# Inverting the chunks of a gated delta rule: 64 columns a level in place of 128

## The chip, the cores and the metric

The kernel runs on one core of a Trainium2 chip. Its time is the device time of one execution in microseconds (us); the median of three runs of the kernel before is 3099.11 us (3098.83 to 3103.76). A core has TensorE (PE: matrix products into the PSUM banks; its weight loads are listed apart as PEld), VectorE (DVE), ScalarE (ACT), GpSimd (POOL), SyncE (SP) and DMA queues. Engines run on their own and wait for each other on semaphores.

## The reference, cut to what matters

One inference step of a two-layer decoder. The first layer is a gated DeltaNet layer of 8 heads on 1024 prompt tokens (and 8 sample tokens), the second a dilated window attention; each is followed by an MLP. In the delta rule the tokens are cut into chunks, and in each chunk a unit lower triangular matrix is inverted:

```python
lower = jnp.where(strict, jnp.einsum('...ik,...jk->...ij', kb, kc) * decay, 0.0)
eye = jnp.broadcast_to(jnp.eye(C, dtype=jnp.float32), lower.shape)
T = lax.linalg.triangular_solve(eye + lower, eye, left_side=True, lower=True, unit_diagonal=True)
u = jnp.einsum('...ij,...jv->...iv', T, vc * bc[..., None])
```

Then a recurrence runs over the chunks with a 128x128 state. All arithmetic is float32.

## The kernel before, in words

The kernel uses chunks of 128 tokens (8 per head, `CH`), which gives the same result as the reference's chunks of 64. For each of the 8 heads each engine runs three functions one after the other: `front` (norms, key products, transposes), `levels` (the inversion) and `recurrence`. TensorE's own order is written out by hand in the program; between the small products of all three functions it runs pieces of the large projection for the next head (`dense`, lines 1854 to 1856: three products of 352 or 328 columns per step), so that it has something to do while the others work. The last head has no such pieces, and has the work for the sample tokens instead (`samples_update`, L1895 on TensorE, L1206 on VectorE).

`levels` inverts by doubling: the inverse of blocks of size b = 2, 4, ..., 64 is known, and a level joins two neighbours of size b into one of 2b (`LEVELS` = 6). `inv` holds the inverse of the 8 chunks, `inv_t` its transpose, `low` the triangular matrices, `blk` what `low` has between the two neighbours of the level (masked by `lvl`), `prod` the first product. The chunks go in two halves h of four chunks, with a PSUM bank for each half. In one level:

- TensorE, L1972 by way of `four` (L1961): for each chunk `blk`^T times `inv`, a float32 product of 128x128 with 128 columns, into bank 3 + h. From level 2 on it also transposes `inv` (L1974, recorded at L1779). Then one step of `dense`.
- ScalarE, L678: copies the bank to `prod`; L683: copies the transpose to `inv_t`.
- TensorE, L1982: `inv_t`^T times `prod` into bank 6 - h (at the last level L1984: `prod`^T times `inv_t` into banks 7 and 3). Then one step of `dense`.
- VectorE, L1317: the next level's `blk`; L1323: subtracts the second product from `inv` (at the last level from `inv_t`). At levels 1 to 4 it also makes the low part of a weight tile (L930), after ScalarE made the high part (L500).

A float32 product appears in the trace as two weight loads and two matmul records; a product of the projection (fp32r) or a transpose as one of each. The first product of level 1 waits for `blk` of L1300, the last step of VectorE's `front`. After level 6 the recurrence waits for the zeroed `state` (L1379), which VectorE writes after its last L1323.

Of the kernel before, what the change touches and what calls it, by code (L numbers as in the profile page):

```python
# [19 lines left out]
ALU = mybir.AluOpType  # L20
# [3 lines left out]
P = 128  # L24
# [150 lines left out]
def build(nc, t):  # L175
# [4 lines left out]
    def sem(name):  # L180
        if name not in made:
            made[name] = ctx.enter_context(nc.semaphore(name))
        return made[name]
# [172 lines left out]
    def hc(h):  # L356
        return slice(4 * h, 4 * h + 4)
# [11 lines left out]
    def conv_out(head, n):  # L369
        return qk(head, n) if n < 2 else v_conv[:]  # L370

    def slots_of(head):
        return ((0, 1), (2, 3))[head % 2]

# [117 lines left out]
    def _(act):  # L492
# [180 lines left out]
        def levels(head):  # L673
            last = head == HEADS - 1
            for level in range(1, LEVELS + 1):
                for h in range(2):
                    act.wait_ge(sem(f"bank{3 + h}_full"), L.next(f"bank{3 + h}_full"))
                    act.activation(prod[:, hc(h)], psum[:, 3 + h].rearrange(four, n=P), ACT.Copy  # L678
                    ).then_inc(sem(f"bank{3 + h}_free"), L.add(f"bank{3 + h}_free"))
                    if level > 1:  # L680
                        b = (7, 5)[h]
                        act.wait_ge(sem(f"bank{b}_full"), L.next(f"bank{b}_full"))
                        act.activation(inv_t[:, hc(h)], psum[:, b].rearrange(four, n=P), ACT.Copy  # L683
                        ).then_inc(sem(f"bank{b}_free"), L.add(f"bank{b}_free"))
                skip(*((6, 5) if level < LEVELS else (7, 3)))
                if not last and level <= 4:
                    which, part = divmod(level - 1, 2)
                    split_hi(2 * head + 4 + which, slots_of(head)[which], (part,))
                if level == 5:
                    act.activation(s_z[:, head], z_g[:, SEQ:NT], ACT.Copy).then_inc(sem("act_order"), L.add("act_order"))  # L690
                    act.activation(z_g[:, 0:SEQ], z_g[:, 0:SEQ], ACT.Silu).then_inc(sem("z_ready"), L.add("z_ready"))
                if last and level == 2:
                    act.wait_ge(sem("s_rows_full"), L.next("s_rows_full"))
                    act.activation(s_rows[:], psum[0:HEADS * NS, 1, 0:2 * P].rearrange("p (k n) -> p k n", n=P), ACT.Copy
                    ).then_inc(sem("s_rows_ready"), L.add("s_rows_ready"))
                    act.wait_ge(sem("s_out_sums_full"), L.next("s_out_sums_full"))
                    act.activation(s_u[:, 6], psum[:, 0, 320:384], ACT.Sqrt, scale=1.0 / P / P, bias=eps[:, 0:1]
                    ).then_inc(sem("s_rms_ready"), L.add("s_rms_ready"))
            if last:
                act.wait_ge(sem("act_order"), L.value("act_order"))  # L700
                act.activation(s_z[:], s_z[:], ACT.Silu).then_inc(sem("s_z_ready"), L.add("s_z_ready"))
# [217 lines left out]
    def _(dve):  # L919
# [387 lines left out]
        def levels(head):  # L1307
            last = head == HEADS - 1
            blk, inv = blk_of(head), inv_of(head)
            for level in range(1, LEVELS + 1):  # L1310
                for h in range(2):
                    v.wait_ge(sem(f"bank{3 + h}_full"), L.next(f"bank{3 + h}_full"))
                    L.skip(f"bank{3 + h}_free")
                if level > 1:
                    skip(7, 5)
                if level < LEVELS:
                    v.tensor_tensor(blk, low[:], o3(lvl[:, level + 1], CH), ALU.mult  # L1317
                    ).then_inc(sem("blocks_ready"), L.add("blocks_ready"))
                v.wait_ge(sem(L.last), L.value(L.last))
                for h in range(2):  # L1320
                    b, to = ((7, 3)[h], inv_t) if level == LEVELS else (6 - h, inv)
                    v.wait_ge(sem(f"bank{b}_full"), L.next(f"bank{b}_full"))
                    v.tensor_tensor(to[:, hc(h)], to[:, hc(h)], psum[:, b].rearrange(four, n=P),  # L1323
                                    ALU.subtract).then_inc(sem(f"bank{b}_free"), L.add(f"bank{b}_free"))
                if not last and level <= 4:
                    which, part = divmod(level - 1, 2)
                    split_lo(2 * head + 4 + which, slots_of(head)[which], (part,))
                if level == 5:
                    v.wait_ge(sem("q_squares_ready"), L.next("q_squares_ready"))
                    for h in range(2):  # L1330
                        v.tensor_reduce(col[:, 1, hc(h)], v_conv[:, halves[h]].rearrange(four, n=P), AXX, ALU.add
                        ).then_inc(sem("dve_order"), L.add("dve_order"))
                    v.wait_ge(sem(L.last), L.value(L.last))
                    v.tensor_scalar(col[:, 4], col[:, 1], EPS, None, ALU.add).then_inc(sem("dve_order"), L.add("dve_order"))
                    v.wait_ge(sem(L.last), L.value(L.last))
                    v.reciprocal(col[:, 11], col[:, 4]).then_inc(sem("dve_order"), L.add("dve_order"))
                if not last and level == 5:
                    take_product(0, head + 1)
                if last and level == 2:
                    samples_values()  # L1340
                if last and level > 2:
                    samples_update(level - 3)
            v.wait_ge(sem(L.last), L.value(L.last))
# [396 lines left out]
    def _(pe):  # L1740
# [217 lines left out]
        def four(bank, h, lhs, rhs):  # L1958
# [2 lines left out]
                done = mm(psum[:, bank, c * P:(c + 1) * P], lhs[:, 4 * h + c], rhs[:, 4 * h + c], start=True, stop=True)  # L1961
            done.then_inc(sem(f"bank{bank}_full"), L.add(f"bank{bank}_full"))

        def levels(head):
            last = head == HEADS - 1
            blk, inv = blk_of(head), inv_of(head)
            at_step = 24
            for level in range(1, LEVELS + 1):
                pe.wait_ge(sem("blocks_ready"), L.next("blocks_ready"))
                for h in range(2):  # L1970
                    peek((5, 7)[h] if level == 1 else 6 - h)
                    four(3 + h, h, blk, inv)  # L1972
                    if level > 1:
                        transposes((7, 5)[h], [inv[:, 4 * h + c] for c in range(4)])  # L1974
                dense(head, at_step, at_step + 1)
                if level == 1:
                    pe.wait_ge(sem("inverse_t_ready"), L.next("inverse_t_ready"))
                for h in range(2):
                    peek(3 + h)
                    peek((7, 5)[h])  # L1980
                    if level < LEVELS:
                        four(6 - h, h, inv_t, prod)  # L1982
                    else:
                        four((7, 3)[h], h, prod, inv_t)  # L1984
                dense(head, at_step + 1, at_step + 2)
                at_step += 2
                if last and level == 1:
                    pe.wait_ge(sem("s_qk_ready"), L.next("s_qk_ready"))
                    pe.wait_ge(sem("s_state_landed"), L.next("s_state_landed", 32))
                    for n in range(HEADS * NS):  # L1990
                        mm(psum[:, 0, 128 + 2 * n:130 + 2 * n], s_state[n // 32][:, n // NS % 4, n % NS], s_u[:, 0:2, n],
                           start=True, stop=True)
                    mm(psum[:, 0, 256:320], ones[:], s_u[:, 2], start=True, stop=True
                    ).then_inc(sem("s_reads_full"), L.add("s_reads_full"))
                if last and level == 2:
                    pe.wait_ge(sem("s_v_ready"), L.next("s_v_ready"))
                    mm(psum[0:HEADS * NS, 1, 0:P], s_u[:, 1], ident[:], start=True, stop=True)
                    mm(psum[0:HEADS * NS, 1, P:2 * P], s_u[:, 5], ident[:], start=True, stop=True
                    ).then_inc(sem("s_rows_full"), L.add("s_rows_full"))
                    pe.wait_ge(sem("s_out_squares_ready"), L.next("s_out_squares_ready"))  # L2000
                    mm(psum[:, 0, 320:384], ones[:], s_u[:, 7], start=True, stop=True
                    ).then_inc(sem("s_out_sums_full"), L.add("s_out_sums_full"))
                if last and level > 2:
                    samples_update(level - 3)
# [333 lines left out]
```

## Time and profile before

| | before |
|---|---|
| median of 3 runs | 3099.11 us |
| the profiled execution | 3105.82 us, its span 3104.0 us |
| mean granted TensorE clock | 0.951 of full speed |
| TensorE busy | 2853.4 us (92%) |
| TensorE weight loads busy | 2779.5 us (90%) |
| VectorE busy | 1664.5 us (54%) |
| ScalarE busy | 858.4 us (28%) |
| DMA | 165.99 MB, mean 53 GB/s |

The span runs from the first to the last instruction. Busy time counts a stretch once however many instructions overlap in it. Matmul records overlap, so what one costs in a stream is the distance between starts, not its own duration. The granted clock (PEclk) is 1.00 at 2.4 GHz and 0.50 at 1.2 GHz. The eight heads (counted from 0) take the stretch from about 84 to about 930 us.

### The profile page before, as it was taken

To read this page: it belongs to the slowest core of one execution; us is meant where nothing else is said; L and a number is where in the kernel's file an instruction comes from. 1 tells how busy PE (TensorE), PEld (TensorE's weight loads), DVE (VectorE), ACT (ScalarE), POOL (GpSimd) and SP (SyncE) were. 2 spreads that over 40 slices of the span, in tenths; PEclk is the share of its full clock that TensorE was granted. 3 is DMA by queue.
4 is the path that set the end of the run, shared out by engine and by line. 5 is a ranking of instruction groups with operands and counts; after the bars stand their busy time and mean duration, and the time that the engine had idled before them with its cause. 6 is when DMAs were issued, how large, how long until landed. Compare 5 with 4: busy or idle time off the path is not lost. (4 is left out here: it accounts for less than half of the span.)

```text
span 3104.0 us, 47551 instructions
## 1 busy us (share of the span) xinstructions
PE 2853.4 (92%) x18652; PEld 2779.5 (90%) x18652; DVE 1664.5 (54%) x3124; ACT 858.4 (28%) x1907; POOL 30.2 (1%) x20
## 2 busy tenths in 40 slices
PE   5999999999777999999999999668849999999998
PEld 2999999999747999999999999658739999999997
DVE  4766677766334644444444653257857444444445
ACT  3544344434112311122111320125514111122111
POOL 0000000000020000000000000000000000000000
PEclk8999999999768999999999999879969999999999
DMA  3100011002113111111111113721231111111111
GB/s 113 55 16 29 29 35 36 29 15 83 62 55 106 55 41 41 54 41 54 41 46 49 41 65 95 68 76 56 76 115 41 55 41 41 54 41 54 41 41 55
DMA packets 102203, 165.99 MB, mean 53 GB/s; under 512 B 47081, under 2 KB 65809, under 8 KB 101604
## 3 DMA queue, kind: packets, MB, share of 16 engines
q1 hardware_dynamic: 59604, 142.35, 14.2%
q10 hardware_dynamic: 42464, 21.74, 3.3%
q8 instruction: 98, 1.61, 0.2%
q14 instruction: 37, 0.30, 0.0%
HBM read 134.63 MB, written 34.67 MB: 55 GB/s over the span
## 5 line engine op out<-in xcount | busy, mean ns | idle before, releaser
L1752 PE MATMUL psum<-x_hi,w_hi 128*128 128x352 f32 (+1 forms) x2128 | 685.8, 322 | 13.4 <-DVE w_lo L930 6.5
L1753 PE MATMUL psum<-x_lo,w_hi 128*128 128x352 f32 (+1 forms) x2128 | 681.2, 320 | 0.0
L1754 PE MATMUL psum<-x_hi,w_lo 128*128 128x352 f32 (+1 forms) x2128 | 677.9, 319 | 0.0
L1752 PE MATMUL psum<-u_hi,w_hi 128*128 128x352 f32 (+1 forms) x1632 | 525.4, 322 | 2.4 <-DVE u_lo L1726 2.4
L1753 PE MATMUL psum<-u_lo,w_hi 128*128 128x352 f32 (+1 forms) x1632 | 522.8, 320 | 0.0
L1754 PE MATMUL psum<-u_hi,w_lo 128*128 128x352 f32 (+1 forms) x1632 | 521.2, 319 | 0.0
L1752 PEld LDWEIGHTS psum<-x_hi,w_hi 128*128 128x128 f32 x2128 | 400.5, 188 | 17.4 <-DVE x L1441 8.7
L1753 PEld LDWEIGHTS psum<-x_lo,w_hi 128*128 128x128 f32 x2128 | 401.0, 188 | 0.7
L1754 PEld LDWEIGHTS psum<-x_hi,w_lo 128*128 128x128 f32 x2128 | 400.7, 188 | 0.0
L776 ACT ACTIVATE u_hi<-relu 128x352 fp32r<-128x352 f32 (+1 forms) x192 | 94.4, 492 | 1047.0 <-DVE relu L1472 1047.0
L1441 DVE TENSOR_TENSOR x<-x,psum 128x352 f32<-128x352 f32 x336 | 170.8, 512 | 363.5 <-PE psum L1754 363.5
L500 ACT ACTIVATE w_hi<-w_raw,gains 128x512 fp32r<-128x512 f32 x384 | 249.2, 712 | 238.6 <-DMA w_raw<-in_w 128.9
L1752 PEld LDWEIGHTS psum<-u_hi,w_hi 128*128 128x128 f32 x1632 | 307.7, 189 | 3.2 <-issue 2.8
L1753 PEld LDWEIGHTS psum<-u_lo,w_hi 128*128 128x128 f32 x1632 | 308.3, 189 | 0.4
L1754 PEld LDWEIGHTS psum<-u_hi,w_lo 128*128 128x128 f32 x1632 | 307.6, 188 | 0.0
L930 DVE SCALAR_TENSOR_TENSOR w_lo<-w_raw,gains,w_hi 128x512 fp32r<-128x512 f32 x384 | 264.0, 746 | 39.3 <-ACT w_hi L500 39.0
L1854 PE MATMUL psum<-x_hi,w_hi 128*128 128x352 f32 (+1 forms) x768 | 273.0, 355 | 12.7 <-issue 10.1
L1855 PE MATMUL psum<-x_lo,w_hi 128*128 128x352 f32 (+1 forms) x768 | 247.5, 322 | 0.0
L1856 PE MATMUL psum<-x_hi,w_lo 128*128 128x352 f32 (+1 forms) x768 | 247.0, 322 | 0.0
L1469 DVE SCALAR_TENSOR_TENSOR relu<-psum,rs 128x352 f32<-128x352 f32 (+1 forms) x192 | 99.1, 516 | 221.5 <-PE psum L1754 216.7
L1854 PEld LDWEIGHTS psum<-x_hi,w_hi 128*128 128x128 f32 x768 | 147.3, 192 | 13.0 <-issue 10.2
L1475 DVE TENSOR_TENSOR u_lo<-relu,u_hi 128x352 fp32r<-128x352 f32 (+1 forms) x192 | 99.3, 517 | 107.1 <-ACT u_hi L776 107.1
(296 smaller groups left out, 3549.7 us busy)
## 6 DMA issues: line engine op xcount, KB each, us to landing
w_raw<-in_w SPq DMA_DIRECT2D x192, 512.0 KB, 3.7
scratch_att<-o_out ACTq DMA_DIRECT2D x48, 132.0 KB, 2.6
q_tile<-scratch_q SPq DMA_DIRECT2D x24, 256.0 KB, 2.9
merge<-scratch_att SPq DMA_DIRECT2D x8, 768.0 KB, 4.7
scratch_q<-q_stage ACTq DMA_DIRECT2D x24, 176.0 KB, 2.3
x<-in_x SPq DMA_DIRECT2D x8, 516.0 KB, 8.1
scratch_o_heads<-head_out ACTq DMA_DIRECT2D x8, 512.0 KB, 2.7
s_state<-in_s_rec_in ACTq DMA_DIRECT2D x2, 2048.0 KB, 10.3
```

Source lines behind the costliest of these rows:

```text
L500: done = act.activation(w_hi[:, slot, 2 * part + k], w_raw[:, part, k], ACT.Copy, scale=gains[:, bass.ds(unit * UW + 2 * part + k, 1)])
L776: act.activation(u_hi[:, tile, THIRDS[third]], relu[:, 0:width(third)], ACT.Copy).then_inc(sem("u_hi_ready"), L.add("u_hi_ready"))
L930: done = v.scalar_tensor_tensor(w_lo[:, slot, 2 * part + k], w_raw[:, part, k], gains[:, bass.ds(unit * UW + 2 * part + k, 1)], f(w_hi[:, ...
L1441: v.tensor_tensor(out, out, psum[:, TAKES[n % 6], 0:width(third)], ALU.add).then_inc(sem("product_free"), L.add("product_free"))
L1469: v.scalar_tensor_tensor(r, psum[:, TAKES[n % 6], 0:width(third)], 0.0, rs[:, cols], ALU.max, ALU.mult).then_inc(sem("product_free"), L.ad ...
L1475: v.tensor_tensor(u_lo[:, tile, cols], r, f(u_hi[:, tile, cols]), ALU.subtract).then_inc(sem("u_ready"), L.add("u_ready"))
L1752: mm(out, whi, xh[:, k, cols], start=k == 0, stop=False)
L1753: mm(out, whi, xl[:, k, cols], start=False, stop=False)
L1754: done = mm(out, wlo, xh[:, k, cols], start=False, stop=k == kts - 1)
L1854: mm(out, whi, x_hi[:, k, cols], start=k == 0, stop=False)
L1855: mm(out, whi, x_lo[:, k, cols], start=False, stop=False)
L1856: done = mm(out, wlo, x_hi[:, k, cols], start=False, stop=k == KT - 1)
```

## The change

The inverse is block triangular. At a level with block size b only the columns of the even blocks (64 of 128) of each chunk's `inv` change. The new kernel computes only these. `upper` picks them: runs of b columns, with b columns left out between them. The first product takes them as moving operand and puts them side by side in the bank; ScalarE copies 64 columns per chunk in place of 128; the second product takes 64 columns; VectorE subtracts 64 columns into the same runs of `inv`. At the last level the roles are swapped: the stationary operand is the 64 columns of `prod`, the moving operand the right half of `inv_t`, and the output 64 partitions with 64 columns. The stationary operand of all other products (`blk`, `inv_t`) stays 128x128. The transposes of `inv`, the copy to `inv_t`, the masks and the order of all instructions stay as they are, and no wait is added or removed.

```diff
+    def upper(ap, level):
+
+        b = 2 ** level
+        return ap.rearrange("p c (n m) -> p c n m", m=2 * b)[:, :, :, 0:b]
...
-                    act.activation(prod[:, hc(h)], psum[:, 3 + h].rearrange(four, n=P), ACT.Copy
+                    act.activation(prod[:, hc(h), 0:P // 2], psum[:, 3 + h, 0:HALF // 2].rearrange(four, n=P // 2), ACT.Copy
                     ).then_inc(sem(f"bank{3 + h}_free"), L.add(f"bank{3 + h}_free"))
...
-                    b, to = ((7, 3)[h], inv_t) if level == LEVELS else (6 - h, inv)
+                    b = (7, 3)[h] if level == LEVELS else 6 - h
                     v.wait_ge(sem(f"bank{b}_full"), L.next(f"bank{b}_full"))
-                    v.tensor_tensor(to[:, hc(h)], to[:, hc(h)], psum[:, b].rearrange(four, n=P),
-                                    ALU.subtract).then_inc(sem(f"bank{b}_free"), L.add(f"bank{b}_free"))
+                    if level < LEVELS:
+                        to = upper(inv[:, hc(h)], level)
+                        new = psum[:, b, 0:HALF // 2].rearrange("p (c n m) -> p c n m", c=4, m=2 ** level)
+                    else:
+                        to = inv_t[0:P // 2, hc(h), P // 2:P]
+                        new = psum[0:P // 2, b, 0:HALF // 2].rearrange(four, n=P // 2)
+                    v.tensor_tensor(to, to, new, ALU.subtract).then_inc(sem(f"bank{b}_free"), L.add(f"bank{b}_free"))
...
+        def halves_of(bank, h, level, lhs, rhs):
+
+            pe.wait_ge(sem(f"bank{bank}_free"), L.next(f"bank{bank}_free"))
+            for c in range(4):
+                cols = slice(c * P // 2, (c + 1) * P // 2)
+                if rhs is not prod and lhs is not prod:
+                    moving = upper(rhs[:, 4 * h + c:4 * h + c + 1], level).rearrange("p c n m -> p (c n) m")
+                    out = psum[:, bank, cols].rearrange("p (n m) -> p n m", m=2 ** level)
+                    done = mm(out, lhs[:, 4 * h + c], moving, start=True, stop=True)
+                elif rhs is prod:
+                    done = mm(psum[:, bank, cols], lhs[:, 4 * h + c], rhs[:, 4 * h + c, 0:P // 2], start=True, stop=True)
+                else:
+                    done = mm(psum[0:P // 2, bank, cols], lhs[:, 4 * h + c, 0:P // 2], rhs[:, 4 * h + c, P // 2:P],
+                              start=True, stop=True)
+            done.then_inc(sem(f"bank{bank}_full"), L.add(f"bank{bank}_full"))
...
-                    four(3 + h, h, blk, inv)
+                    halves_of(3 + h, h, level, blk, inv)
...
-                        four(6 - h, h, inv_t, prod)
+                        halves_of(6 - h, h, level, inv_t, prod)
                     else:
-                        four((7, 3)[h], h, prod, inv_t)
+                        halves_of((7, 3)[h], h, level, prod, inv_t)
```

## Rows read from the trace of the kernel before

**Rows 1.** Waits of TensorE, 84 to 785 us: engine, line, releaser: us, times, longest.
```profile
PE psum L1961 <- DVE pair L1300: 15.4, 7, 2.2
PE psum L2021 <- DVE state L1379: 3.9, 7, 0.6
```
**Rows 2.** Windows, head 1: levels, then the rest: PE, PEld, DVE, ACT, POOL, PEclk, DMA.
```profile
222.56:255.00 32.44, 31.88 (x269) 31.60 (x269) 22.59 (x33) 17.96 (x32) 0.00 (x0) 1.00 0.22 66
255.00:317.00 62.00, 59.80 (x430) 59.51 (x431) 43.30 (x88) 24.04 (x62) 0.00 (x0) 1.00 0.03 10
```
**Rows 3.** Timeline of TensorE, one level of head 2: start, us, engine, line, count.
```profile
321.85 1.05 PE L1961 MATMUL psum<-pair 128*128 128x128 f32 x8
322.74 0.60 PE L1779 MATMUL psum<-ident,pair 128*128 128x128 f32 x4
323.18 1.06 PE L1961 MATMUL psum<-pair 128*128 128x128 f32 x8
...
325.00 1.95 PE L1961 MATMUL psum<-dec,inv_t 128*128 128x128 f32 x16
326.70 0.41 PE L1854 MATMUL psum<-x_hi,w_hi 128*128 128x352 f32 x1
```
**Rows 4.** Timeline of TensorE, four short streams with other operand sizes.
```profile
42.87 3.57 PE L1793 MATMUL psum<-ones,sq_sum 128*128 128x1 f32 x16 [4.93 <-DVE sq_sum L952]
52.01 0.60 PE L1871 MATMUL psum<-x,w_ab 128*16 128x8 f32 x16
802.67 27.44 PE L1991 MATMUL psum<-s_u,s_state 128*128 128x2 f32 x128 [6.86 <-DMA s_state<-in_s_rec_in]
1026.18 0.71 PE L1806 MATMUL psum<-ones,sq_sums 128*88 128x1 f32 x8
1026.75 0.39 PE L1752 MATMUL psum<-x_hi,w_hi 128*128 128x328 f32 x1
```
**Rows 5.** Timeline of TensorE, the last head's level 1.
```profile
789.91 3.62 PE L1961 MATMUL psum<-pair 128*128 128x128 f32 x16
793.32 2.49 PE L1961 MATMUL psum<-dec,inv_t 128*128 128x128 f32 x16
```
**Rows 6.** Groups of VectorE and ScalarE in the heads: count, busy us, mean ns, idle before.
```profile
L1323 DVE TENSOR_TENSOR pair<-pair,psum 128x512 f32<-128x512 f32 x70 | 48.1, 688 | 25.3 <-PE psum L1961 20.1
L1277 DVE TENSOR_TENSOR low<-psum,pair 128x256 f32<-128x256 f32 x32 | 13.3, 414 | 0.3 <-PE psum L1921 0.2
L678 ACT ACTIVATE dec<-psum 128x512 f32<-128x512 f32 x96 | 57.3, 597 | 182.0 <-PE psum L1961 182.0
L694 ACT ACTIVATE s_rows<-psum 64x256 f32<-64x256 f32 x1 | 0.4, 377 | 3.5 <-PE psum L1998 3.5
```
**Rows 7.** Timeline of TensorE, from level 6 to the recurrence, head 2.
```profile
346.65 1.95 PE L1961 MATMUL psum<-inv_t,dec 128*128 128x128 f32 x16
348.36 0.41 PE L1854 MATMUL psum<-x_hi,w_hi 128*128 128x352 f32 x1
```
**Rows 8.** Timeline of TensorE, first product of four heads' levels.
```profile
127.91 2.95 PE L1961 MATMUL psum<-pair 128*128 128x128 f32 x16 [2.20 <-DVE pair L1300]
222.56 2.05 PE L1961 MATMUL psum<-pair 128*128 128x128 f32 x16 [2.20 <-DVE pair L1300]
315.60 2.91 PE L1961 MATMUL psum<-pair 128*128 128x128 f32 x16 [2.20 <-DVE pair L1300]
410.26 2.05 PE L1961 MATMUL psum<-pair 128*128 128x128 f32 x16 [2.20 <-DVE pair L1300]
```
**Rows 9.** Windows: after the gap of head 2, twice; then the sample products; the last recurrence.
```profile
316.60:320.00 3.40, 3.40 (x17) 3.40 (x16) 1.23 (x1) 2.05 (x4) 0.00 (x0) 0.50 0.02 7
320.00:349.60 29.60, 29.08 (x247) 28.79 (x245) 20.57 (x30) 15.91 (x29) 0.00 (x0) 1.00 0.24 72
802.70:830.10 27.40, 27.40 (x129) 27.40 (x129) 0.00 (x0) 0.00 (x0) 0.00 (x0) 0.50 0.00 1
880.00:925.00 45.00, 40.18 (x95) 22.68 (x93) 16.69 (x43) 4.96 (x22) 14.97 (x8) 0.50 0.16 63
```
**Rows 10.** Windows: the last head's levels 2 to 6.
```profile
835.50:876.40 40.90, 32.77 (x196) 25.80 (x194) 18.24 (x28) 12.91 (x24) 14.98 (x8) 0.87 0.07 26
```

## The prediction

> **What bounds the kernel now.** I read the waits of TensorE first, since it is busy 92% of the span. Between 84 and 785 us, seven heads long, it waits for VectorE twice per head and for next to nothing else: 2.20 us at the door of the levels and about 0.56 us at the door of the recurrence, 19.3 us in 700 [rows 1]. The windows say the same: in a head's levels TensorE is busy 31.88 of 32.44 us, while VectorE has 22.59 and ScalarE 17.96 [rows 2]. So in seven heads the time is the length of TensorE's own stream. What an operation costs there is the distance from its first start to the next group's start: in a level, 8 records of the first product take 0.89 us, 4 transposes 0.44, 16 records of the second product 1.70 [rows 3]: 107 to 111 ns a record. The last head has no projection to fill in, and there TensorE also waits for VectorE [rows 10].
>
> **The change part by part.** *The products.* Per head 6 levels x 2 halves x 4 chunks x 2 products x 2 records = 192 records get 64 moving columns in place of 128. Does a record get shorter? The trace has streams with nearly no moving columns. With a 128-column stationary operand, 128 records of 2 moving columns take 27.3 us (802.67 to 829.97), 213 ns each, at a granted clock of 0.50 [rows 4, 9]. At the same clock 16 records of 128 moving columns take 3.41 us, 213 ns each [rows 5]. Sixteen records of 1 column with 128 stationary columns: the last ends 3.57 us after the first began [rows 4], the same pace. At full clock 8 records with 88 stationary columns and 1 moving take 0.57 us, 71 ns each, which is 88/128 of 107 less 2 ns; and with 16 stationary columns and 8 moving a record costs under 38 ns (0.60 us for 16) [rows 4]. So the pace of these records goes by the stationary columns: the weight load takes the whole slot, and the moving columns run inside it. 176 of the 192 records keep 128 stationary columns, and I forecast 107 to 111 ns for them, as before. The bounds for one record: 107 (all load) and 53 (half). I take the upper end, because two streams of 1 and 2 columns lie on it and 64 is between them and 128. What is unseen is a moving operand in runs of 2 or 4 elements with gaps: it has half the slot as slack, so even at twice the time per column it costs nothing; at four times, levels 1 and 2 would cost 64 records x 0.1 us x 8 heads = 26 us at most.
>
> The 16 records of the second product at level 6 have 64 stationary and 64 moving columns: 107 ns becomes 53, 0.86 us per head at full clock.
>
> The Trainium skill (TensorE: Matmul & The Clock Gate, "Back-to-back issue gap") has the gap between matmuls shrink with the moving columns, down to about 60 cycles at 64. By that alone all 192 records would halve; it is the third rival below. The trace's streams of 1 and 2 columns disagree with it for float32 operands with 128 stationary columns [rows 4].
>
> *The copies and subtractions.* L1323 goes from 688 ns to that of L1277, which also takes 256 elements from a bank: 414. 12 of them per head: 3.3 us less of VectorE. L678 goes from 597 towards 377 (L694, 256 elements): 2.6 us less of ScalarE per head [rows 6]. Both lie beside TensorE's stream, which doesn't wait for them [rows 1], so they are worth nothing in seven heads but for one place: after level 6 TensorE waits for L1379, which stands behind the last two L1323. There the second product ends 0.86 us sooner, the step of the projection behind it still takes its time [rows 7], and VectorE is 0.27 us faster per subtraction: I take 0.27 us per head (0 to 0.55). If the runs of 2 elements double the price of a subtraction, it is 0.83 us, near the 0.69 of before, and stays hidden. Nothing is added, moved or made to wait.
>
> So a head gains 0.86 + 0.27 = 1.13 us so long as the clock stays. The 2.20 us at the door of the levels stay too: their releaser is in `front`.
>
> *The clock.* This is the term that decides. At the door of the levels TensorE stands 2.20 us, in all seven heads alike. In four of them (the first, third, fifth and seventh) the granted clock then falls to 0.50: the first product is 2.9 us long in place of 2.05 [rows 8]. About 1 us after that product's start the clock is down, and after 3.4 us of back-to-back work it is up again and stays for the level [rows 9]. A fall costs 1.61 us (the heads' first products lie 94.65, 93.04, 94.66 us apart) [rows 8]. What brought it back was a stream of full 128-column and 352-column records. Other streams don't bring it back, though TensorE is busy: 27.40 us busy out of 27.40 at 0.50 with 2 moving columns, and the last recurrence, 40.18 busy out of 45.00 at 0.50, with gaps and half-filled products [rows 9]. After the change the levels are such a stream: of the 10 us that a level takes at half clock, 6.8 are records whose moving columns fill half their slot. I forecast that a fall at the door now lasts through all levels, until the recurrence with its many 352-column records raises the clock. Also, a fall becomes likelier, since what follows the gap is thin too.
>
> The Trainium skill (same page, "Part 1: The HAM clock gate") says that matmul activity releases the throttle and asks to keep TensorE busy. If busy time as the profile shows it were that activity, the clock would come back within the levels as before; this is the second rival. The rows of 27.40 and 40.18 busy us at 0.50 speak against it.
>
> Price of one fall: the levels hold 31.88 us of TensorE's work [rows 2]. At half clock all of it doubles except the 16 records that halved: (31.9 - 1.7) x 2 + 1.7 = 62.1, so +30.2. Less 1.0 before the clock is down; plus some 5 us (3 to 7) of recurrence still at half clock, +2.5; less 0.3 at the recurrence's door: +31.4 us.
>
> How many falls? Before, four of seven, in strict alternation, because the heads are of nearly equal length. A head that is 31 us longer and others 1.1 us shorter break that pattern. The same 2.20 us made the clock fall at one door and not at the next, so something that the rows don't show decides. I take three of seven, next to the four of the rows, and one to five as bounds.
>
> *The last head.* Its level 1 ends long before the sample state lands (6.86 us of waiting) [rows 4] and can get slower for nothing. From there it starts at half clock; now the first full records raise the clock, 0.87 on average over levels 2 to 6, which means 30 of 40.9 us at full clock, some 24 of them busy [rows 10]. With thin records it stays down: at most +24. VectorE's shorter subtractions on the chain to L1895 give back 2. I take +17 (10 to 24).
>
> Sum: 3 x 31.4 = +94.3; the four falls of before gone, -6.4; four heads at full clock, 4 x 1.13 = -4.5; last head +17: **+100 us**. The profiled execution, 3105.8 us, would be 3206; it is 6.7 above the median of the runs, against which the forecast is 3099.1 + 100 = 3199 us.
>
> **The rivals.**
> - *The clock falls, but comes back within the levels*, helped by the transposes and the projection's steps: a third of a level's time at half clock is filled with full records. Then a fall costs perhaps 10 us: 3 x 10 + 10 for the last head - 14 = +26, 3125 us.
> - *The clock behaves as before* (busy time is what counts). Then only the gains are left: 8 x 0.86 + 8 x 0.27 = 9, and 2 of VectorE's chain in the last head: -11, 3088 us, faster. For it: the levels' stream has no gap. Against: rows 9. It decides from the point where no door's fall outlasts the few us of now.
> - *Records halve with their columns*: 1408 more records save 50 ns each, -70, together 3018 us. Against: rows 4.
> - *Runs with gaps are slow to read or write*: +26 at most, inside the forecast's range.
>
> **How the numbers follow.** Forecast 0.74; clock comes back within the levels 0.08; clock as before 0.12; records halve 0.06. A measurement of this kernel tells 0.2%, 6 us. Faster: the last two, less a little, 0.17. Same, 0.06: no fall at any door and the last head's +17 against -11 of gains. Slower 0.77. With one to five falls the forecast itself reaches from 3130 to 3260, and single executions should differ by tens of us, since the door's gap decides anew in each. The range is 3088 to 3250: it takes in the clock as before, and leaves out halved records and more than four or five falls.
>
> **What would show it.** Right: starts of the 64-column records 107 to 111 ns apart at full clock and 213 at half, level 6's second product 53 and 107; long stretches of PEclk 0.50 over whole `levels`, about 64 us long in place of 32.4, and a lower mean clock (0.951 now, near 0.92); L1323 near 414 ns; executions of one kernel that differ by more than the 5 us of now. Wrong: a level of under 5 us at full clock (records did halve), or PEclk 0.50 for only some 3 us behind each door.

## The result and the profile after

The changed kernel takes 3131.41 us (median of four runs, 3126.46 to 3142.18), the kernel before 3101.44 (3098.83 to 3105.89): ratio 1.010, 95% interval 1.0067 to 1.0133. It is slower by 30 us. The forecast was slower by 100. Its four runs lie 15.7 us apart, those of before 7.1. The profiled executions below (3105.82 and 3142.18 us) are at the long end of both kernels.

| | before | after |
|---|---|---|
| the profiled execution | 3105.82 us | 3142.18 us |
| its span | 3104.0 us | 3140.4 us |
| mean granted TensorE clock | 0.951 | 0.933 |
| TensorE busy | 2853.4 us | 2895.9 us |
| VectorE busy | 1664.5 us | 1635.6 us |
| ScalarE busy | 858.4 us | 845.9 us |

TensorE has less to stream and is busy for longer. Where, the windows of the changed kernel say, from the first product of the levels to the first product of the recurrence, one line for each head (stretch, its length, PE, PEld, DVE, ACT and POOL busy with counts, PEclk, DMA share, GB/s):

```profile
127.84:173.33 45.49, 45.24 (x268) 44.83 (x268) 19.39 (x33) 16.48 (x32) 0.00 (x0) 0.66 0.16 47
233.95:271.36 37.41, 37.16 (x268) 36.75 (x268) 19.40 (x33) 16.49 (x32) 0.00 (x0) 0.82 0.20 57
331.99:367.79 35.80, 35.56 (x268) 35.14 (x268) 19.40 (x33) 16.49 (x32) 0.00 (x0) 0.86 0.19 60
428.41:465.82 37.41, 37.16 (x268) 36.75 (x268) 19.39 (x33) 16.49 (x32) 0.00 (x0) 0.82 0.19 57
526.44:560.63 34.19, 33.94 (x268) 33.53 (x268) 19.39 (x33) 16.48 (x32) 0.00 (x0) 0.90 0.20 62
621.25:652.22 30.97, 30.72 (x268) 30.30 (x268) 19.40 (x33) 16.49 (x32) 0.00 (x0) 1.00 0.23 69
712.83:750.26 37.43, 37.18 (x268) 36.76 (x268) 19.39 (x33) 16.49 (x32) 0.00 (x0) 0.82 0.49 169
814.84:919.10 104.26, 90.19 (x386) 78.62 (x386) 19.27 (x39) 15.38 (x30) 14.97 (x8) 0.52 0.14 56
```

The same windows of the kernel before, for a head without a fall of the clock, one with (there are three and four of them), and the last head:

```profile
222.31:254.74 32.43, 31.87 (x268) 31.58 (x268) 22.67 (x33) 17.96 (x32) 0.00 (x0) 1.00 0.22 66
315.35:349.39 34.04, 33.48 (x268) 33.19 (x268) 22.67 (x33) 17.96 (x32) 0.00 (x0) 0.95 0.21 64
...
789.66:880.58 90.92, 73.88 (x386) 65.29 (x385) 24.77 (x39) 17.29 (x30) 14.98 (x8) 0.71 0.16 64
```

The head with PEclk 1.00 is 1.46 us shorter than before (30.97 against 32.43). In the six others the clock falls. A length times (1 - PEclk) times 2 gives the time at half clock: 31, 13, 10, 13, 7, 0 and 13 us, 88 in all, against 14 before. What it costs is what a window has above 30.97: 14.5, 6.4, 4.8, 6.4, 3.2, 0 and 6.5 us, 41.9 in all, a little under half of the 88 us. The four falls of before cost 4 x 1.61 = 6.4, and the shorter stream gives back 7 x 1.46 = 10.2, so the seven windows are 41.9 - 6.4 - 10.2 = 25.3 us longer (258.7 us in all). The last head's levels are 13.3 us longer, and the stretch behind them 2.1 us shorter. Together that is the 36.4 us by which the span grew.

The three other executions of the changed kernel have mean clocks of 0.936 to 0.939 against 0.933 in the profiled one. By their spans this is 20 to 40 us less at half clock (an estimate; where in the kernel, no run shows). So what is read from this profile is the upper end of what the change costs: 36 us, where the medians say 30.

The timeline of TensorE in the changed kernel shows parts of two levels at half clock (first five lines, head 0), then a whole level at full clock, then level 6's second product (start, us, engine, line, count):

```profile
135.38 1.80 PE L1982 MATMUL psum<-pair 128*128 128x64 f32 x8
136.97 1.06 PE L1789 MATMUL psum<-ident,pair 128*128 128x128 f32 x4
137.82 1.81 PE L1982 MATMUL psum<-pair 128*128 128x64 f32 x8
...
151.24 3.51 PE L1984 MATMUL psum<-dec,inv_t 128*128 128x64 f32 x16
154.51 0.64 PE L1864 MATMUL psum<-x_hi,w_hi 128*128 128x352 f32 x1
...
163.20 1.00 PE L1982 MATMUL psum<-pair 128*128 128x64 f32 x8
164.04 0.61 PE L1789 MATMUL psum<-ident,pair 128*128 128x128 f32 x4
...
166.26 1.89 PE L1984 MATMUL psum<-dec,inv_t 128*128 128x64 f32 x16
167.96 0.41 PE L1864 MATMUL psum<-x_hi,w_hi 128*128 128x352 f32 x1
168.52 1.00 PE L1982 MATMUL psum<-pair 128*128 128x64 f32 x8
...
171.67 1.15 PE L1986 MATMUL psum<-inv_t,dec 128*64 128x64 f32 x16
172.74 0.43 PE L1864 MATMUL psum<-x_hi,w_hi 128*128 128x352 f32 x1
```

At full clock 8 records with 64 moving columns take 0.84 us (163.20 to 164.04) where 8 with 128 took 0.89 [rows 3]; 16 of the second product take 1.70 us, as before. A whole level takes 5.32 us (163.20 to 168.52) against 5.41. Half the columns are gone, and 0.09 us of 5.41 with them. At half clock 8 records take 1.59 us (135.38 to 136.97), 199 ns each, and 16 of the second product 3.27 (151.24 to 154.51), 204 ns each.

### The profile page after: what moved, and what is told of

Read it like the earlier page. It is cut to its first block and busy times, and to the rows that moved or that the text cites. A ratio compares the mean times of both kernels' runs of the same rounds, so it can differ in the third digit from the quotient of the medians.

```text
span 3140.4 us, 47551 instructions
## 1 busy us (share of the span) xinstructions
PE 2895.9 (92%) x18652; PEld 2818.3 (90%) x18652; DVE 1635.6 (52%) x3124; ACT 845.9 (27%) x1907; POOL 30.1 (1%) x20
## 3 DMA queue, kind: packets, MB, share of 16 engines
q8 instruction: 98, 1.61, 0.2%
```

## The experiments

Each was timed beside the kernel before on the same chip; ratios are to that.

**1. The gap at the door filled, changed kernel.** Four steps of the projection, which the recurrence had, are issued where TensorE stands idle.

```diff
+DOOR = 4
...
-            at_step = 24
+            at_step = 24 + DOOR
+            dense(head, 24, at_step)
...
-            start = 24 + 2 * LEVELS
+            start = 24 + DOOR + 2 * LEVELS
```

> The changed kernel, with four of the projection's steps moved from the recurrence to the door of the levels, where TensorE stands 2.20 us idle in each of seven heads. Theory (the slowdown is the clock, which falls at that idle stretch and which the thin records then hold down): four steps are 1.9 us, so 0.3 us of idling is left, the clock doesn't fall in heads 0 to 6, their levels run at full clock, 1.5 us shorter than before, and the idle time filled gives 1.9 us more per head: 7 x -3.4 = -24 us against the kernel before, +13 for the last head, which has no projection to fill in: about 3090 us. Rival (records with gaps in their moving operand, or the small copies, cost the time): the clock may rise, but the time stays at 3131 less 13, near 3118.

Measured: 3093.09 us (3085.05 to 3094.71) beside 3107.85 before, ratio 0.9943 (0.9929 to 0.9956). The windows of the levels, first of seven like ones and the last head:

```profile
129.19:160.15 30.96, 30.71 (x268) 30.29 (x268) 19.40 (x33) 16.51 (x32) 0.00 (x0) 1.00 0.24 69
...
761.02:865.55 104.53, 90.59 (x386) 79.11 (x385) 19.29 (x39) 15.40 (x30) 14.97 (x8) 0.52 0.14 56
```

PEclk is 1.00 in all seven heads, and the same thin stream (one whose records have few moving columns for the slot of 128) takes 30.96 us there. So 64-column records alone didn't make the clock fall in these heads; the idle stretch was needed for it, though it was not enough by itself: in the changed kernel one of seven doors kept the clock, before the change three. The last head, with no step to fill in, is as long as in the changed kernel. The slowdown of the seven heads is the clock's, and not that of the operands with gaps. Beside their own times before, the changed kernel is 30 us slower with the gap and 15 us faster without it: 45 us, some 6 per door.

**2. The same move in the kernel before.**

> The kernel before with the same move of four steps, the control for the first run. Theory: the idle time filled gives 7 x 1.9 = 13 us, and the four falls of the clock (1.6 us each) go: -20, about 3081 us, so the first run is then some 10 us above this one, all of it from the last head. Rival (the recurrence lacks the four steps and waits there): 3095 to 3101 us, with new waits of TensorE in the recurrence.

Measured: 3088.73 us (3087.27 to 3091.03), ratio 0.9940 (0.9926 to 0.9953): 19 us faster than before. Its seven windows are 32.42 or 32.43 us long at PEclk 1.00, so the four falls are gone. In its waits of TensorE the door is down to 1.9 us in total for seven heads, and the recurrence shows no new wait:

```profile
PE psum L2023 <- DVE state L1380: 3.9, 7, 0.6
PE psum L1962 <- DVE pair L1301: 1.9, 7, 0.3
```

The move is worth 19 us alone, as expected (20; the absolute 3081 was missed because the kernel before ran 6 us longer beside these runs). The change adds nothing to it: the seven heads gain 10 us by the change and the last head loses 13.8 (104.53 against 90.73). The first run is 4.4 us above this one by medians. I had expected some 10, because my expectation for the first run left out the four falls that go.

**3. Level 1 at 128 columns, the rest of the change kept.** In all three engines `level == 1` takes the old form.

```diff
-                    halves_of(3 + h, h, level, blk, inv)
+                    if level == 1:
+                        four(3 + h, h, blk, inv)
+                    else:
+                        halves_of(3 + h, h, level, blk, inv)
```

> The changed kernel, but level 1, which lies right behind the idle stretch, keeps its 128 columns in both products, the copy and the subtraction. Theory: the full records of level 1 bring the clock back as they did before (3.4 us at half clock per fall), and levels 2 to 6 are thin at full clock: falls in about four of seven heads, at 1.6 us each; seven heads 9 us shorter than before, the last head 13 longer: about 3105 us. Rival (the clock comes back only in the projection's and the transposes' records, whatever level 1 does): 3125 to 3131 us and 10 us at half clock per head.

Measured: 3109.26 us (3102.36 to 3112.93, 11 runs), ratio 1.0003 (0.9994 to 1.0012). The windows: five heads like the first line, two like the second, then the last head:

```profile
129.13:160.09 30.96, 30.71 (x268) 30.30 (x268) 19.93 (x33) 16.93 (x32) 0.00 (x0) 1.00 0.21 69
...
403.89:436.44 32.55, 32.30 (x268) 31.88 (x268) 19.93 (x33) 16.93 (x32) 0.00 (x0) 0.95 0.23 65
...
777.68:875.22 97.54, 82.63 (x386) 73.54 (x385) 21.02 (x39) 15.82 (x30) 14.97 (x8) 0.59 0.15 59
```

A fall costs 1.6 us again, as before the change. In this execution one full level behind the gap was enough to bring the clock back, and five thin levels after it then ran at full clock. The last head is 6.6 us longer than before, not the 13 expected. This profile is of the shortest of the eleven executions; most of the others have lower mean clocks (down to 0.944 against 0.948), so they had more or longer stretches at half clock, and the median is 7 us above it. Even so, the median of all eleven is 1 us above the kernel before, where the changed kernel's is 30.

**4. VectorE's part alone.** All products and copies at 128 columns, the subtraction on 64.

```diff
+                    bank = psum[:, b].rearrange(four, n=P)
+                    if level < LEVELS:
+                        to, new = upper(to[:, hc(h)], level), upper(bank, level)
+                    else:
+                        to, new = to[0:P // 2, hc(h), P // 2:P], bank[0:P // 2, :, P // 2:P]
```

> The kernel before with VectorE's part alone: all products and the copies at 128 columns, the subtraction L1323 on the 64 columns that change. Theory: a subtraction takes about 414 ns in place of 688; worth 0.5 us per head at the recurrence's door and 2 us on the chain of the last head: 3096 us, mean clock 0.95 as before. Rival (subtractions in runs of 2 elements are slow): L1323 over 688 ns at levels 1 and 2, and no gain.

Measured: 3100.93 us (3096.36 to 3106.00) beside 3107.85, ratio 0.9974 (0.9964 to 0.9985), clock 0.953. The levels are 32.15 us long against 32.43, the last head's 89.18 against 90.92. That is 2.0 and 1.7 us of the 6.9; and in its profile two doors fell, not four, which is 3.2 us more by way of the clock. So the expected 0.5 us per head at the recurrence's door was 0.28. The subtraction takes 421 ns here (413 at level 6) in place of 688. The shortest and the longest of the 80 at levels 1 to 5 are 414 and 432 ns, so runs of 2 elements cost no more than runs of 32. The changed kernel's groups of VectorE show the same times:

```profile
L1334 DVE TENSOR_TENSOR pair<-pair,psum 128x256 f32<-128x256 f32 x70 | 29.5, 421 | 51.4 <-PE psum L1984 51.3
L1334 DVE TENSOR_TENSOR inv_t<-inv_t,psum 64x256 f32<-64x256 f32 x14 | 5.5, 413 | 13.0 <-PE psum L1986 13.0
```

**5. The parts that pay, together.** The kernel before with the door filled, VectorE's part, and of the products only level 6's second:

```diff
+        def corner(bank, h):
...
+                done = mm(psum[0:P // 2, bank, c * P // 2:(c + 1) * P // 2], prod[:, 4 * h + c, 0:P // 2],
+                          inv_t[:, 4 * h + c, P // 2:P], start=True, stop=True)
```

> The kernel before with the parts that the first runs showed to be worth something: four projection steps at the door, VectorE's subtraction on 64 columns, and level 6's second product as 64 stationary and 64 moving columns; all other products and the copies stay at 128 columns, so that no record is thin for its slot. Theory: the door-filled kernel before (3088.7) less 7 for VectorE's part and 8 x 0.86 for level 6: 3075 us, levels of heads 0 to 6 33.6 us long, no fall of the clock there, the last head's levels no longer than before (94 us). Rival (thin records save something themselves, so that leaving 11 of 12 products full loses it): no better than the door-filled changed kernel, 3090.

Measured: 3073.23 us (3072.53 to 3075.30) beside 3103.68, ratio 0.9905 (0.9889 to 0.9920). It is 30 us faster than before. The changed kernel with its door filled was 15 us faster than its own before, so this one is 12 (by the ratios) to 16 us (by the medians) better; the two ran on different chips, and their times can't be subtracted directly. Levels, first of seven like ones, and the last head:

```profile
127.27:158.71 31.44, 31.20 (x268) 30.78 (x268) 19.39 (x33) 17.97 (x32) 0.00 (x0) 1.00 0.24 68
...
762.50:851.15 88.65, 72.43 (x386) 64.60 (x385) 21.51 (x39) 17.20 (x30) 14.97 (x8) 0.73 0.16 64
```

A level stretch is 0.48 us longer than the all-thin one (30.96), and the last head 15.9 us shorter. The time came out as expected (3075), the parts less so: level 6's second product gives 0.63 us and not 0.86, and the last head's levels are 2.3 us shorter than before. The 33.6 us expected for a level stretch compare with 31.44 plus the 1.9 of the four steps, which stand ahead of this window.

**6. 32 moving columns.** The changed kernel with both products of levels 1 to 5 and the first of level 6 at 32 columns; half of what a level changes is left out.

```diff
...
-                    done = mm(psum[:, bank, cols], lhs[:, 4 * h + c], rhs[:, 4 * h + c, 0:P // 2], start=True, stop=True)
+                    done = mm(psum[:, bank, c * P // 2:c * P // 2 + P // 4], lhs[:, 4 * h + c], rhs[:, 4 * h + c, 0:P // 4],
+                              start=True, stop=True)
```

> The changed kernel with 32 moving columns in place of 64 in both products of levels 1 to 5 and in the first of level 6 (it leaves out half of what each level changes). Theory (the pace goes by the stationary columns, and how thin the records are decides how long the clock stays down): records at full clock still 107 to 111 ns apart; falls at about as many doors, but each now lasts to the end of the levels, some 30 us lost per fall: 3150 to 3250 us, and runs far apart. Rival 1 (the pace goes by the moving columns after all, with a floor): records under 90 ns apart and a shorter level. Rival 2 (the clock comes back by time or by busy share alone): falls as long as in the changed kernel, about 14 us at half clock, 3131 us.

Measured: 3283.07 us (3279.24 to 3289.52), ratio 1.0574 (1.0558 to 1.0591). The two kinds of head alternate, and none keeps the clock; then TensorE's timeline inside one:

```profile
128.71:185.09 56.38, 56.14 (x267) 55.64 (x268) 19.44 (x33) 16.51 (x32) 0.00 (x0) 0.52 0.13 38
245.71:303.18 57.47, 57.22 (x268) 56.71 (x268) 19.61 (x34) 16.50 (x32) 0.00 (x0) 0.51 0.12 37
```
```profile
266.77 1.75 PE L1983 MATMUL psum<-pair 128*128 128x32 f32 x8
268.33 1.09 PE L1789 MATMUL psum<-ident,pair 128*128 128x128 f32 x4
...
270.11 3.46 PE L1985 MATMUL psum<-dec,inv_t 128*128 128x32 f32 x16
273.37 0.64 PE L1864 MATMUL psum<-x_hi,w_hi 128*128 128x352 f32 x1
```

A quarter of the columns, and a record still takes 195 to 204 ns at half clock (1.56 us for 8, 3.26 for 16), where one of 64 columns takes 199 to 204. The pace is not the moving columns'. And here a fall lasts to the end of the levels, at every door: both rivals are out. The time lies above the range that I gave. A fall costs 25.4 or 26.5 us (over 30.96), less than the 30 expected, but all seven doors fell, which is 181 us. The runs are 10 us apart and not far apart as expected.

**7. 64 stationary columns in the second product** of levels 1 to 5 of the changed kernel; the update of the lower 64 rows is left out.

```diff
-                    done = mm(psum[:, bank, cols], lhs[:, 4 * h + c], rhs[:, 4 * h + c, 0:P // 2], start=True, stop=True)
+                    done = mm(psum[0:P // 2, bank, cols], lhs[:, 4 * h + c, 0:P // 2], rhs[:, 4 * h + c, 0:P // 2],
+                              start=True, stop=True)
```

> The changed kernel with 64 stationary columns in place of 128 in the second product of levels 1 to 5 (it leaves out the update of the lower 64 rows). Theory: these 640 records go 53 to 57 ns apart at full clock in place of 107 to 111, and they fill their slot again: 5 x 16 x 0.054 = 4.3 us less per head at full clock, 30 in seven heads, 2 to 4 in the last; half clock per fall shorter than the changed kernel's 14 us: 3131 - 30 - 3 - some 10 for the clock = 3088 us. Rival (64 columns run no faster; level 6 was short for another reason): 3131 us.

Measured: 3093.42 us (3082.85 to 3098.36) beside 3103.68, ratio 0.9971 (0.9959 to 0.9983). TensorE's timeline, second product at full clock, and two of the windows:

```profile
228.90 1.14 PE L1984 MATMUL psum<-dec,inv_t 128*64 128x64 f32 x16
229.97 0.43 PE L1864 MATMUL psum<-x_hi,w_hi 128*128 128x352 f32 x1
```
```profile
216.57:244.98 28.41, 28.16 (x268) 26.32 (x268) 19.21 (x33) 16.49 (x32) 0.00 (x0) 1.00 0.26 75
...
666.30:697.80 31.50, 31.25 (x268) 29.18 (x268) 19.30 (x33) 16.49 (x32) 0.00 (x0) 0.89 0.57 198
```

With the same 64 moving columns but 64 stationary ones, 16 records take 1.07 us in place of 1.70: here the stream does get shorter, though 67 ns a record is more than the 53 to 57 expected. Four of seven doors fall (PEclk 0.94 and 0.89, two of each), for 3.4 and 6.9 us. This too is the shortest execution, 9 to 16 us below the five others (mean clock 0.947 against 0.942 or 0.943), so in the others the stretches at half clock were more or longer. Experiments 6 and 7 leave work out and so compute other values; no run separates the values from the column counts.

**8. The last head at 128 columns**, the others as changed (each form chosen by `last`).

> The changed kernel with 128 columns for everything in the last head's levels. Theory: the last head's levels, 108 us in the changed kernel's profile against 95 before, are 95 again, and heads 0 to 6 stay as changed: 13 us less, 3118 us. Rival (the last head is longer for what comes before it): 3131 us.

Measured: 3126.80 us (3123.17 to 3128.25), ratio 1.0073 (1.0060 to 1.0087). The windows of the first three heads and of the last:

```profile
128.90:169.55 40.65, 40.41 (x268) 39.99 (x268) 19.40 (x33) 16.48 (x32) 0.00 (x0) 0.75 0.17 53
230.17:261.13 30.96, 30.72 (x268) 30.30 (x268) 19.40 (x33) 16.49 (x32) 0.00 (x0) 1.00 0.23 69
321.75:359.17 37.42, 37.17 (x268) 36.75 (x268) 19.41 (x33) 16.48 (x32) 0.00 (x0) 0.82 0.20 58
...
812.70:904.88 92.18, 74.28 (x386) 66.10 (x386) 24.61 (x39) 17.25 (x30) 14.97 (x8) 0.72 0.16 62
```

In the profile it is 12.1 us shorter than in the changed kernel, as expected. In the times the gain is some 7 us, and the interval overlaps that of the changed kernel, so the size of this part rests on the profile. Heads 0 to 6 have the changed kernel's stream, so this is a second view of its falls: again six doors of seven, for 10 to 20 us each, and the seven windows have 38.8 us above 30.96, where the changed kernel's have 41.9.

## Why the prediction was wrong in size

- *TensorE's stream sets the time; copies and subtractions are hidden*: right in the main. VectorE's part alone gave 0.26%, of which nearly half, by its profile, is two falls fewer (experiment 4).
- *Records keep their pace, since the weight load with its 128 columns takes the slot*: right to some 6% (0.84 and 1.70 us in place of 0.89 and 1.70; at half clock 199 to 204 ns a record in place of 213), and shown from both sides: 32 moving columns shorten a record no further than to 195, 64 stationary ones do shorten it (experiments 6 and 7). That it is the weight load which fills the slot is the likeliest reading, not a measured one. The third rival is out, and so is the fourth: the stream in runs with gaps takes 30.96 us. One row was misread: the records with 16 stationary columns ran at half clock (PEclk 0.50 from 52.00 to 52.60 us), so their 38 ns belong beside 213 and not beside 107. The conclusion stands without them.
- *Level 6's second product*: 1.07 us in place of 1.70; I had 0.86 less, it is 0.63. The door of the recurrence gave 0.31 for 0.27: the wait for L1379 is gone from the list, and TensorE's idle time in a window falls from 0.56 to 0.25. With the 0.09 per level, a head at full clock gains 1.46 in place of 1.13.
- *The clock decides, and falls at the door*: right (experiments 1 and 3). A fall became likelier: six doors of seven, in two profiles; I had taken three.
- *The last head +17*: 13.3 by the windows.
- **The step that failed** is "a fall at the door now lasts through all levels", priced at 31.4 us a fall. In the profile a fall lasts 7 to 31 us, 14.7 on average, and costs 7.0: the clock came back inside the levels every time, in the first head after 31 of its 45 us. Six falls at 7.0 are 42 us where the sum had three at 31.4, 94. The rest of the sum was near (-6.4, about -10 and +13 for -6.4, -4.5 and +17). So it is my first rival, "comes back within the levels", to which I gave 0.08 with 26 us, that came true. That its 26 us lie so near the measured 30 is in part luck: it had three falls at 10, and there were six at 7.

Why it was mis-sized: the rows showed two ends, streams of 1 and 2 moving columns that stay at half clock and streams of 128 that come back after 3.4 us [rows 9], and I put 64 at the low end. The experiments lay out what is between. Time at half clock per fall, each from one profile: 128 columns behind the door 3.4 us (experiment 3); 64 stationary columns in the second product 3.4 to 6.9 (7); 64 moving columns in a slot for 128, 7 to 31 (the change, and 8); 32, to the end of the levels, 54 to 56 us in each head (6: 56.38 x 0.48 x 2 = 54, 57.47 x 0.49 x 2 = 56). Only with 32 columns does a fall do what I had forecast for 64, and even there it costs 25.4 to 26.5 us and not 31.4.

The Trainium skill (TensorE: Matmul & The Clock Gate, "Part 1: The HAM clock gate") says that activity releases the throttle. Busy time as the profile counts it was not enough for that here: in experiment 6 TensorE is busy 56.14 of 56.38 us at a mean granted clock of 0.52.

Open stays what makes one fall of the same stream last 7 us and another 31, and which doors fall in a given execution. No run here separates that. The rows show only that the costs go in steps: the seven windows of the change have 9, 4, 3, 4, 2, 0 and 4 times the 1.61 us that one fall cost before.

## What to carry to other kernels

Halving the moving columns of a float32 product saved next to nothing here, where the stationary operand keeps 128 columns (0.09 us of 5.41 a level); look for a row with few moving columns and the same stationary width before counting on it, and cut the stationary side instead. An idle stretch of 2 us in front of a thin stream cost far more than 2 us, some 6 per door: it is the gap that is to be filled, from work that stands later, and that alone was worth 19 us before the change and 45 after it. Where a stream must be thin, keep the part right behind an idle stretch full: level 1 at 128 columns took the change from +30 us to +1.

## What the runs showed of the hardware that was not expected

- A thin stream has a graded effect: with 64 moving columns it did not lower the clock from full (30.96 us at 1.00 in seven heads), and took 7 to 31 us to raise it from half; with 32 it did not raise it in 54 us.
- A float32 record with 64 stationary and 64 moving columns goes at 67 ns at full clock (1.07 us for 16), not at half of 107.
- At half clock records of 64 and 32 moving columns go at 195 to 204 ns, below the 213 of those with 128 [rows 5] and of those with 2 [rows 4]. The same place in a level, 8 records of the first product, shows it too: 1.59 us with 64 columns (135.38 to 136.97) and 1.70 us with 128, in the last head of the kernel before:

```profile
833.10 1.91 PE L1961 MATMUL psum<-pair 128*128 128x128 f32 x8
834.80 0.90 PE L1779 MATMUL psum<-ident,pair 128*128 128x128 f32 x4
```
